# Forming the modulation columns of a two-block network on TensorE with wide moving operands

## The reference

```python
cond = jax.nn.silu(c)
for i in range(DEPTH):
    mod = cond @ ada_w[i] + ada_b[i]                  # ada_w[i]: 1024 x 3072
    shift, scale, gate = jnp.split(mod[:, None, :], 3, axis=-1)
    h = rmsnorm(x, norm_w[i]) * (1 + scale) + shift
    y = gdn_mixer(h, ...) if i % 2 == 0 else fox_mixer(h, ...)   # begin with h @ w_in
    x = x + gate * y
```

## Time and profile before

| | us |
|---|---|
| median of three runs | 1749.95 |
| lowest, highest | 1748.53, 1750.89 |
| the profiled execution | 1745.44 |
| its span, first to last instruction | 1743.7 |
| TensorE busy in it | 1667.5 |

### The profile page before, as it was taken

The page is one execution under the profiler, slowest core; times in us unless marked ns, Lnnn a source line. Parts: engine busy times, 40 slices in busy tenths (PEclk is TensorE's granted clock), DMA queues, the critical chain, the costliest instruction groups (busy, mean ns, idle before and its releaser), DMA issues.

```text
span 1743.7 us, 34471 instructions
## 1 busy us (share of the span) xinstructions
PE 1667.5 (96%) x11737; PEld 1547.4 (89%) x11737; DVE 1178.3 (68%) x2361; ACT 922.7 (53%) x1713; POOL 434.6 (25%) x344
## 2 busy tenths in 40 slices
PE   8999989999999988999999999999999999999998
PEld 8999768888988877989999999989999988888886
DVE  3676378887545556548646999979888755555554
ACT  1665523333345555456444444469898755555554
POOL 3000024423000000400003777776666400000000
PEclk9999989999999999999999999999999999999999
DMA  9555410110934433533653555555454465555653
GB/s 297 174 189 180 133 49 25 48 48 25 289 98 146 121 109 104 169 109 109 186 129 108 167 167 172 168 158 144 135 144 127 149 198 192 193 192 193 193 193 132
DMA packets 211808, 255.54 MB, mean 147 GB/s; under 512 B 15911, under 2 KB 193803, under 8 KB 211723
## 3 DMA queue, kind: packets, MB, share of 16 engines
q1 hardware_dynamic: 211723, 254.39, 47.9%
HBM read 253.29 MB, written 1.05 MB: 146 GB/s over the span
## 4 chain that ended last, share of the span: by engine, by line
PE 75%; DVE 10%; DMA 5%; issue 4%; ACT 3%; SPq 2%; DVEq 0%; ACTq 0%
PE ps L2023 21%; PE ps L2563 20%; PE ps L2545 9%; DMA raw<-in_u_experts 4%; PE ps L2533 3%; PE ps L2043 2%; PE ps L2185 2%; DVE raw L1794 2%; PE ps L2064 2%; PE ps L2276 2%; SPq L547 2%; PE ps L2196 2%; PE ps L2197 2%; PE ps L2117 1%; PE ps L2343 1%
## 5 line engine op out<-in xcount | busy, mean ns | idle before, releaser
L675 POOL TENSOR_TENSOR w_lo<-raw,w_hi 128x1024 fp32r<-128x1024 f32 x128 | 307.6, 2407 | 334.5 <-ACT w_hi L1131 334.5
L2023 PE MATMUL ps<-x_hi,w_hi 128*128 128x256 f32 x1088 | 314.0, 289 | 6.6 <-DVE w_lo L1253 3.0
L2023 PE MATMUL ps<-x_lo,w_hi 128*128 128x256 f32 x1088 | 309.6, 285 | 0.0
L2023 PE MATMUL ps<-x_hi,w_lo 128*128 128x256 f32 x1088 | 309.5, 284 | 0.0
L1982 DVE TENSOR_TENSOR w_lo<-raw,w_hi 128x1024 fp32r<-128x1024 f32 x124 | 152.0, 1226 | 143.2 <-ACT w_hi L1231 143.2
L1231 ACT ACTIVATE w_hi<-raw 128x1024 fp32r<-128x1024 f32 x124 | 131.6, 1061 | 168.0 <-PE ps L2563 168.0
L2023 PEld LDWEIGHTS ps<-x_hi,w_hi 128*128 128x128 f32 x1088 | 210.4, 193 | 10.3 <-issue 3.9
L2023 PEld LDWEIGHTS ps<-x_lo,w_hi 128*128 128x128 f32 x1088 | 210.7, 194 | 0.3 <-issue 0.2
L2023 PEld LDWEIGHTS ps<-x_hi,w_lo 128*128 128x128 f32 x1088 | 210.4, 193 | 0.0
L1131 ACT ACTIVATE w_hi<-raw 128x1024 fp32r<-128x1024 f32 x128 | 134.9, 1054 | 118.9 <-DVE raw L1794 118.8
L2508 PE MATMUL ps<-x_hi,w_hi 128*128 128x256 f32 x576 | 166.5, 289 | 9.8 <-ACT arena L1153 9.7
(11 more groups left out here) (394 smaller groups left out, 3880.5 us busy)
## 6 DMA issues: line engine op xcount, KB each, us to landing
raw<-in_u_experts SPq DMA_DIRECT2D x512, 128.0 KB, 2.7
raw<-in_v_experts SPq DMA_DIRECT2D x128, 512.0 KB, 4.3
arena<-in_ada_w SPq DMA_DIRECT2D x22, 1024.0 KB, 5.2
raw<-in_a_w_in SPq DMA_DIRECT2D x12, 1024.0 KB, 5.3
arena<-in_a_w_in SPq DMA_DIRECT2D x12, 1024.0 KB, 5.4
raw<-in_b_w_in SPq DMA_DIRECT2D x8, 1024.0 KB, 5.5
arena<-in_b_w_in SPq DMA_DIRECT2D x8, 1024.0 KB, 5.8
raw<-in_w_in SPq DMA_DIRECT2D x8, 1024.0 KB, 5.5
```

What stands on the lines that cost most here:

```text
L675: pool.tensor_tensor(UTL[e], UT[e % 2], UTH[e].bitcast(F32), ALU.subtract).then_inc(utl_ready, 1)
L2023: ins = mm(o[:, b * S:b * S + S], w[:, slot, kk, b * P:b * P + P], xx[:, (kk + turn) % KC, :], start=(kk == 0 and n == 0), stop=(kk == k - ...
```

## The change

- TensorE forms all eight modulation tiles in one way: `CONDR` is the weights, and the tile moves, 256 columns at a time, 8 matmuls per tile, into PSUM bank 0 or 1 in turn. Every row of the bank then holds the 256 sums.
- VectorE turns each into two columns (`to_columns`): it multiplies the bank with the identity, kept in the new buffer `DIAG`, and sums along the row into `MC`. A tile may start when VectorE has read the tile two before it (`ada_free`).
- The weighted sums on VectorE are gone. CONDR is written first thing. On VectorE to_columns(0) to (3) stand in front of `x_ready`, and (4) to (7) behind the norm. On TensorE tiles 0 to 4 stand ahead of the norm's transposes and tiles 5 to 7 behind.
- SP loads the first projection tile behind modulation tile 4, in front of 5, 6 and 7.
- The counts of `mod_sum` and `ada_free` that others wait for are adjusted (lines 639, 754, 2172 and the like).

```diff
@@ -343,12 +343,12 @@
         ROWS = [ps[6], ps[7]]
         OS = [[XX[p_][g_][:, 0:256] for g_ in range(2)] for p_ in range(2)]
         VS = [[XX[p_][g_][:, 256:512] for g_ in range(2)] for p_ in range(2)]
+        DIAG = two(at(26880, 256))
         GATEW = [at(4096 + 2048 * u, 2048).rearrange("p (k n) -> p k n", k=KC) for u in range(4)]
 
         ADA_W = RAW + GATEW
         ada_in = raw_in + [gate_in, fn_in, wg_in, sk_in]
         COND8 = AR[0:8, T0 + 256:T0 + 384]
-        MODS = ps[6][:, 0:16]
 
         aq = T0 + 4096
         aSQ, aRN = at(aq, 512), at(aq + 512, 512)
@@ -461,10 +461,10 @@
             ada(2)
             ada(3)
             sp.dma_start(X, x.rearrange("b (a p) n -> p (b a) n", p=P)).then_inc(x_in, 16)
-            for u in range(4, 7):
+            ada(4)
+            load(T_AIN, 0, 0, a_w_in[0], 0)
+            for u in range(5, 8):
                 ada(u)
-            load(T_AIN, 0, 0, a_w_in[0], 0)
-            ada(7)
             load(T_AIN, 0, 1, a_w_in[0], TW)
             sp.wait_ge(cond_ready, 1)
             sp.dma_start(rowf, attn_sinks).then_inc(rows_in, 16)
@@ -1296,28 +1296,30 @@
                     v.scalar_tensor_tensor(X[:, t, :], X[:, t, :], rstd[:, t:t + 1], w, ALU.mult, ALU.mult).then_inc(nt_row, 1)
 
             v.sem_inc(bank_free, 2)
-            v.sem_inc(ada_free, 6)
+            v.sem_inc(ada_free, 2)
+            v.wait_ge(cond_ready, 1)
+            v.tensor_copy(CONDR[:, :, :], condT.unsqueeze(2).broadcast_to([P, KC, P])).then_inc(cond_ready, 1)
+            def to_columns(n):
+
+                v.wait_ge(raw_free, 4 + n + 1)
+                if n:
+                    v.wait_ge(mod_sum, n)
+                v.tensor_tensor(DIAG, two(ps[n % 2][:, 0:TW]), bcast(ident, 2), ALU.mult).then_inc(ada_free, 1)
+                v.wait_ge(ada_free, n + 3)
+                v.tensor_reduce(MC[:, 2 * n:2 * n + 2], DIAG, AX_X, ALU.add).then_inc(mod_sum, 1)
+
+            to_columns(0)
             v.wait_ge(cols_T, 2)
             v.tensor_copy(COLS, ps[2][:, 0:238]).then_inc(cols_ready, 1)
-            v.wait_ge(cond_ready, 1)
-
-            def weighted_sum(n, blocks, done):
-
-                w, first = ADA_W[n], blocks[0]
-                v.wait_ge(ada_in[n], 16)
-                v.tensor_scalar(w[:, first, :], w[:, first, :], condT[:, first:first + 1], None, ALU.mult).then_inc(mod_sum, 1)
-                for j, kk in enumerate(blocks[1:]):
-                    v.wait_ge(mod_sum, done + j + 1)
-                    v.scalar_tensor_tensor(w[:, first, :], w[:, kk, :], condT[:, kk:kk + 1], w[:, first, :],
-                                           ALU.mult, ALU.add).then_inc(mod_sum, 1)
-
-            weighted_sum(2, range(8), 0)
-            v.tensor_copy(CONDR[:, :, :], condT.unsqueeze(2).broadcast_to([P, KC, P])).then_inc(cond_ready, 1)
+            for n in (1, 2, 3):
+                to_columns(n)
             v.wait_ge(x_in, 16)
             v.sem_inc(x_ready, 1)
             norm(0)
-            weighted_sum(6, range(8), 8)
-            weighted_sum(7, range(4, 8), 16)
+            to_columns(4)
+            to_columns(5)
+            to_columns(6)
+            to_columns(7)
 
             def modulation(l, shift, scale, n):
 
@@ -1327,15 +1329,15 @@
                 v.wait_ge(mod_cols, n + 2)
                 v.tensor_tensor(NSC[:, l, :], NSC[:, l, :], COLS[:, CN + 8 * l:CN + 8 * l + 8], ALU.mult).then_inc(mod_cols, 1)
 
-            v.wait_ge(mod_T, 1)
+            v.wait_ge(mod_sum, 8)
             v.wait_ge(cols_ready, 1)
-            modulation(0, MODS[:, 0:8], MODS[:, 8:16], 0)
+            modulation(0, MC[:, 0:8], MC[:, 8:16], 0)
             v.wait_ge(mod_cols, 3)
 
             def scaled(k):
                 v.wait_ge(nt_T, k // 2 + 1)
                 v.tensor_scalar(H[:, k, :], bo_block(k), NSC[:, 0, k:k + 1], NSH[:, 0, k:k + 1],
-                                ALU.mult, ALU.add).then_inc(ada_free, 1)
+                                ALU.mult, ALU.add).then_inc(mod_sum, 1)
 
             def low(k):
                 v.wait_ge(nt_h, k + 1)
@@ -1353,7 +1355,7 @@
             v.wait_ge(lo_ready, 1)
             lo(T_AIN, 0, 1)
             lo(T_AIN, 0, 2)
-            v.wait_ge(mod_T, 2)
+            v.wait_ge(mod_T, 1)
             v.wait_ge(rows_in, 16 * 8)
 
             def gates(l, banks):
@@ -2059,41 +2061,31 @@
             pe.transpose(ps[2][:, 0:8], COND8, ident[0:8, 0:8]).then_inc(cols_T, 1)
 
             def modulation(n, blocks):
-                for cc in range(2):
-                    for kk in blocks:
-                        ins = mm(MODS[:, 2 * n + cc:2 * n + cc + 1], ADA_W[n][:, kk, cc * P:cc * P + P], condT[:, kk:kk + 1],
-                                 start=(n == 0 and cc == 0 and kk == 0), stop=(kk == KC - 1), skip_group_check=True)
+                pe.wait_ge(ada_in[n], 16)
+                pe.wait_ge(ada_free, n + 1)
+                for kk in blocks:
+                    ins = mm(ps[n % 2][:, 0:TW], CONDR[:, kk, :], ADA_W[n][:, kk, :], start=(kk == 0), stop=(kk == KC - 1))
                 return ins
 
-            def summed_modulation(n, first, done):
-                pe.wait_ge(mod_sum, done)
-                for cc in range(2):
-                    ins = mm(MODS[:, 2 * n + cc:2 * n + cc + 1], ADA_W[n][:, first, cc * P:cc * P + P], ones[:, 0:1],
-                             start=False, stop=True, skip_group_check=True)
-                return ins
-
-            pe.wait_ge(cond_ready, 1)
-            pe.wait_ge(ada_in[0], 16)
+            pe.wait_ge(cond_ready, 2)
             modulation(0, range(8)).then_inc(raw_free, 1)
             pe.wait_ge(vec_in, 16 * 14)
             pe.transpose(ps[2][:, 0:128], S1, ident)
             pe.transpose(ps[2][:, 128:128 + VEC_ROWS], S2[0:VEC_ROWS, :], ident[0:VEC_ROWS, 0:VEC_ROWS]).then_inc(cols_T, 1)
-            pe.wait_ge(ada_in[1], 16)
             modulation(1, range(8)).then_inc(raw_free, 1)
-            summed_modulation(2, 0, 8).then_inc(raw_free, 1)
-            for n in (3, 4, 5):
-                pe.wait_ge(ada_in[n], 16)
-                modulation(n, range(8)).then_inc(raw_free, 1)
+            modulation(2, range(8)).then_inc(raw_free, 1)
+            modulation(3, range(8)).then_inc(raw_free, 1)
+            modulation(4, range(8)).then_inc(raw_free, 1)
             pe.wait_ge(cols_ready, 1)
             norm(0)
-            summed_modulation(6, 0, 16).then_inc(raw_free, 1)
-            pe.wait_ge(ada_in[7], 16)
-            modulation(7, range(4)).then_inc(raw_free, 1)
-            summed_modulation(7, 4, 20).then_inc(mod_T, 1)
+            modulation(5, range(8)).then_inc(raw_free, 1)
+            modulation(6, range(8)).then_inc(raw_free, 1)
+            modulation(7, range(8)).then_inc(raw_free, 1)
             x_round[0] = 0
             columns_tile(T_AIN, 0, 0)
             pe.wait_ge(rows_in, 16 * 8)
             pe.wait_ge(ada_free, 10)
+            pe.wait_ge(mod_sum, 12)
             pe.wait_ge(nt_h, KC)
             mm(ps[5][:, 0:16], ones[0:1, :], rowf, start=True, stop=True).then_inc(mod_T, 1)
             for kk in range(KC):
```

More of the change, by code:

```diff
@@ L638, in _ @@
                 for half, done in ((4, 8), (2, 12), (1, 14)):
-                    pool.wait_ge(mod_sum, 15 * i + (20 + done))
+                    pool.wait_ge(mod_sum, 15 * i + (12 + done))
                     for kk in range(half):
@@ L753, in high @@
                 if k % 4 < 2:
-                    act.wait_ge(ada_free, 6 + k % 4 + k // 2 + 1)
+                    act.wait_ge(mod_sum, 8 + k % 4 + k // 2 + 1)
                 else:
@@ L2112, in _ @@
             pe.wait_ge(bank_free, 2 + T_AOUT - N_ADA)
-            pe.wait_ge(cond_ready, 2)
             def gate_rows(w, bank, u):
@@ L2171, in modulator @@
                     pe.wait_ge(h_xm, n.nth(0, 1, 0, 2))
-                pe.wait_ge(mod_sum, r.count(15, 20 + 15))
+                pe.wait_ge(mod_sum, r.count(15, 12 + 15))
                 pe.wait_ge(ada_free, r.count(1, 10))
```

## The result

| | before | changed |
|---|---|---|
| median of the first comparison (4 runs each), us | 1749.24 | 1737.89 |
| ratio, 95% interval | | 0.9937 [0.9917, 0.9957] |
| profiled execution, us | 1745.44 | 1741.16 |
| its span, us | 1743.7 | 1739.4 |
| forecast of the median, us | | 1742.5 (1740.0 to 1747.0) |

Three later comparisons gave ratios of 0.9942 [0.9924, 0.9960], 0.9934 [0.9923, 0.9946] and 0.9958 [0.9942, 0.9974]. Over these four the changed kernel has a mean of 1739.3 us (22 executions, standard deviation 2.9), the kernel before 1748.7 us (67 executions, 2.0); three executions in a slow state, of 2644 and 7339 us (kernel before) and 4945 us (experiment 2), are left out. The difference is 9.4 us, give or take 1.3 us.

A forecast was written before the change was run, and what follows sets the result against it. TensorE was taken to bound the kernel, busy 1667.5 of 1743.7 us and alone setting the chain from 6.69 to 48.4 us. Gains of 6.9 + 0.6 = 7.5 us took 1749.95 to 1742.5 us, range 1740.0 to 1747.0.

The forecast's parts named there:

- Narrow matmuls keep the clock down, wide ones bring it up: Modulation tiles: TensorE at 1.2 GHz through one-column matmuls until about 45 us; wide tiles reach 2.4 GHz, 3.46 us each.
- Tile 0 to 12.4 us: First modulation tile: clock rises 4.6 us after its start; ends at 12.4 us (11.9 to 12.9; 13.6 if all slow).
- The new order ahead of the norm: Statistics and norm wait for to_columns(3): norm done at 28.35 us, TensorE idle 1.6 us before the transposes.
- The moved load costs nothing: First projection tile queued behind modulation tile 4: cost 0, tile 5 covered by 0.4 us, waits on raw_free already met.
- Projection at 43.65 us: First projection matmul starts at 43.65 us, 6.9 us earlier than before.
- First projection tile, 0.6 us: First projection tile, 8.59 us before, gets 0.6 us shorter (0 to 1.2), bounded by VectorE splitting x.
- Gain of the head 7.5 us: Start of the program: 6.9 us from the earlier projection plus 0.6 us in its first tile.
- So the rest moves with it: Program behind the first projection tile: TensorE runs gapless at full pace, so the whole gains the head's 7.5 us.
- The clock did not fall between tiles 4 and 5: Reduced-gain rival: clock falls once between tiles 4 and 5; gain 4.6 us, 1745.3 us; chance 0.19.
- rows_in held nothing up: Swallowed-gain rival: matmul behind the first projection tile waits for small transfers (rows_in); gain 3.2 us, 1746.7 us; chance 0.10.
- The slow rival: Clock stays at 1.2 GHz through the wide tiles; projection 18.9 us later, about 1769 us; chance 0.08.
- a transpose does not count as activity for the clock: Skill rule against the forecast: idle time and transposes, 1.6 and 1.9 us, make one pause; tile 5 partly at half clock.

The follow-up runs named there:

- experiment 2: Changed kernel with the first projection tile loaded behind modulation tile 6 again, as before the change: 1742.73 us, ratio 0.9958.
- Experiment 3: Kernel before plus nine dummy 128-column fp32 matmuls while TensorE waits for tile 0: 1746.81 us, ratio 0.9982.
- experiment 5: Changed kernel again, 1738.4 us, ratio 0.9934; and changed kernel with x_ready given before to_columns(3), 1738.23 us, ratio 0.9945.
- the cut kernels: Kernels cut off behind the first projection tile and its tail matmuls: before 69.41 us, changed 62.47 us, changed with idle stretches filled 60.82 us.
- the delayed kernel: Changed kernel plus 29 dummy 128-column fp32 matmuls behind the first projection tile: 1746.75 us, ratio 0.9992.
- experiment 4: Kernel before, unchanged, profiled a third time: 1749.09 us.
- experiment 6: Changed kernel with x_ready early, old load order, nine dummy matmuls ahead of tile 0 and eleven behind tile 7: 1738.58 us, ratio 0.9935.
- experiment 8: Changed kernel again, 1740.29 us; with 29 dummy matmuls behind the first projection tile, 1746.75 us; with idle stretches filled, x_ready early, old load order, 1737.45 us.

## Why the prediction was right, and where it was wrong

**Narrow matmuls keep the clock down, wide ones bring it up: right.** Experiment 3 shows the one-column records at both paces (0.21 and 0.112 us), and the changed kernel the wide ones at 0.216 us. Two readings behind this step were off, without harm. The six instructions at 44 us are transposes and the eleven at 46 us one-column matmuls, so not the same kind of work; what carries the step is that each kind was seen at two paces, the 16 transposes in 3.52 us and in 1.94 us. And the count of a stretch takes in what reaches into it from the one before: 11 in a us are 9 starts, and a narrow tile at full clock takes 3.6 us (2 x 1.79), not 2.9 to 3.2 us.

**Tile 0 to 12.4 us: the mechanism right, its ends too narrow.** Tile 0 ended at 13.14, 12.00, 13.43 and 12.02 us in four profiles, two of them past the 11.9 to 12.9 us given: in these two nearly all of it ran at half clock (6.33 and 6.61 us, where 16 slow records take 6.9 us). Tiles 1 to 3 took their 10.4 us.

**The new order ahead of the norm: right.** ScalarE at 24.29 us, the transposes at 28.64 us (28.35 forecast), 1.46 us of idle time (1.6). VectorE's reduction took 0.42 us where 0.38 us was taken, but ScalarE did not wait for its end.

**The moved load costs nothing: right, but not for every reason given.** Experiment 2 shows that it costs nothing, and GpSimd ran beside to_columns(4) without holding it up. But the wait of the load for tile 0 was not over before its turn came: the SP queue stood still for 1.4 us and sent the load at 13.17 us, right behind the end of tile 0 at 13.14 us. With x_ready early (experiment 5) this wait lies on the chain, and tile 6 comes 0.2 us late.

**Projection at 43.65 us: right.** 44.03, 42.98, 44.31 and 43.05 us in four profiles.

**First projection tile, 0.6 us: too much, within its ends.** It took 8.51, 8.14, 8.79 and 8.09 us, mean 8.4 us, against 8.59 us in the profile that the forecast started from: 0.2 us (0.1 us against the mean of the three profiles of before). That the clock falls around the idle time was right; where it falls moves the tile.

**Gain of the head 7.5 us: right in size.** 6.9 us by the cut kernels (6.6 us in their means), 6.6 us in the first pair of profiles, 7.8 us between the means of all profiles.

**What failed is the step from the head to the whole.** "So the rest moves with it" put the program behind the head at 0 us of gain without a reason but TensorE's full pace, and the range held only the head's own uncertainty, neither the spread of whole executions nor that of the base. The miss of 4.6 us (1742.5 against 1737.89) divides into three parts by the pooled means. The base of 1749.95 us, a median of three, was 1.2 us above the mean of 67 executions. The four executions of the first comparison were 1.4 us below the mean of 22; that much is the luck of the draw. And the gain is 9.4 us (give or take 1.3), not 7.5 us, which leaves 1.9 us. Against the head as measured, 6.6 to 7.8 us, the term put at nothing is 1.6 to 2.8 us.

Of that, 0.5 us is shown, as shorter waits behind the head in every profile of the changed code. The rest is open, and the runs disagree on it: the delayed kernel leaves 0.6 us for the program behind the head, uncertain by 1.5 us; the profiled executions show none of it (1745.9 - 1738.7 = 7.2 us between the mean spans above), though three and four of them can't tell 2 us; and while three comparisons put the gain at 10 to 11 us, the fourth puts it at 7.7 us.

**The rivals.** The clock did not fall between tiles 4 and 5: the three tiles behind the transposes took 10.38 us in every profile of the changed kernel. rows_in held nothing up: the tail matmul followed the projection tile at once. The slow rival was far off. The Trainium skill (TensorE: Matmul & The Clock Gate, Part 4: PE-mode transpose) says that a transpose does not count as activity for the clock; this case's traces are mixed on that. In the first two profiles of the kernel before the clock came up during the transposes, and in experiment 3 too; in the third (experiment 4) it did not; and in the changed kernel 1.46 us of idle time and 1.94 us of transposes behind it left the clock up.

## What to carry to other kernels

Cost a matmul not by its own time alone but by what it does to the clock: here one-column matmuls kept TensorE busy and at half clock for 35 us, and wide ones that need about the same time at full clock (3.46 us a tile against 3.6 us) ran twice as fast for that reason. Where the granted clock is not yet on record, read the pace, and read it from starts or from whole groups, of one kind of instruction. And before a range is given for a change of a few us in a long program, look at how far its executions lie apart and put that into the range: a head measured alone, in a kernel cut off behind it, told 6.6 us to within 1 us with 11 short executions, where 89 whole ones leave 1.3 us of doubt.

## What the hardware showed beyond expectation

- TensorE busy without a break in one-column matmuls lost the clock: up until the end of the 10th us, then 0.50 until 44 us (experiment 3).
- TensorE waits inside a tile (0.72 busy in the 47th us of experiment 6) did not bring the clock down, while 3.1 us of idle time ahead of the tile did.
- Beside GpSimd's 4.5 us instruction a VectorE tensor_scalar lasted 3.63 us in place of 0.35 us, while a tensor_tensor that reads PSUM and a tensor_reduce took their usual 0.42 us each (experiment 2).
- A half clock at the start of the first projection tile, where TensorE depends on VectorE anyway, cost nothing: 7.7 us with it and without it (experiment 6).
- The same waits behind the head came out 0.2 to 0.3 us shorter in all profiles of the changed code (experiment 8).
